# Filling the first block of a two-layer fp32 transformer kernel tile by tile instead of by column halves

## The reference

```
def swiglu(x, w_gate, w_up, w_down):
    return (jax.nn.silu(x @ w_gate) * (x @ w_up)) @ w_down

f1 = swiglu(rms_norm(x, ffn1_pre_g[l]), ffn1_w_gate[l], ffn1_w_up[l], ffn1_w_down[l])
x = x + FFN_RESIDUAL_WEIGHT * rms_norm(f1, ffn1_post_g[l])
m = token_mixer(rms_norm(x, mix_pre_g[l]), w_in[l], ...)
x = x + rms_norm(m, mix_post_g[l])
f2 = swiglu(rms_norm(x, ffn2_pre_g[l]), ffn2_w_gate[l], ffn2_w_up[l], ffn2_w_down[l])
```

## Time and profile before

| what | value |
|---|---|
| median of three runs | 1047.85 us (1047.4 to 1048.85) |
| the profiled execution's own time | 1048.85 us |
| its span | 1047.0 us |
| PE busy | 1030.4 us, 98% |
| DVE busy | 629.5 us, 60% |
| ACT busy | 473.7 us, 45% |
| DMA over the span | 178.78 MB, mean 171 GB/s |

### The profile page before, as it was taken

The page is one execution under the profiler, slowest core; times in us unless marked ns, Lnnn a source line. Parts: engine busy times, 40 slices in busy tenths (PEclk is TensorE's granted clock), DMA queues, the critical chain, the costliest instruction groups (busy, mean ns, idle before and its releaser), DMA issues.

```text
span 1047.0 us, 13589 instructions
## 1 busy us (share of the span) xinstructions
PE 1030.4 (98%) x5026; PEld 855.5 (82%) x5026; DVE 629.5 (60%) x642; ACT 473.7 (45%) x537; POOL 69.8 (7%) x81
## 2 busy tenths in 40 slices
PE   8999999999979999999999999999999999999998
PEld 6888888778867888888888888888888888888887
DVE  6555456655556645455664478876777766544553
ACT  6534445555453634443544542335446445434342
POOL 2000000100110100000010002243000000000000
PEclk9999999999999999999999999999999999999999
DMA  9755657565313455655646543334436555565551
GB/s 311 233 192 184 200 163 230 178 198 176 121 41 120 148 194 180 200 162 198 231 152 201 179 148 116 121 121 153 129 121 201 162 200 190 176 197 190 194 177 41
DMA packets 116664, 178.78 MB, mean 171 GB/s; under 512 B 5640, under 2 KB 73488, under 8 KB 116496
## 3 DMA queue, kind: packets, MB, share of 16 engines
q1 hardware_dynamic: 115808, 174.82, 51.0%
q0 software_dynamic: 512, 1.71, 0.6%
q10 hardware_dynamic: 304, 1.70, 0.6%
HBM read 177.15 MB, written 2.63 MB: 172 GB/s over the span
## 4 chain that ended last, share of the span: by engine, by line
PE 94%; DVE 3%; ACT 2%; issue 1%; DMA 0%; POOL 0%; SPq 0%; ACTq 0%; DVEq 0%; POOLq 0%
PE gu L492 14%; PE gu L493 14%; PE gu L494 14%; PE acc L492 10%; PE acc L494 10%; PE acc L493 10%; PE tp L492 3%; PE tp L494 3%; PE tp L493 3%; PE acc L819 3%; PE tp L631 1%; PE gu L734 1%; PE acc L720 1%; PE tp L533 1%; PE acc L746 1%
## 5 line engine op out<-in xcount | busy, mean ns | idle before, releaser
L1504 DVE TENSOR_TENSOR wlo<-raw,whi 128x2048 fp32r<-128x2048 f32 x149 | 346.1, 2326 | 188.7 <-ACT whi L1018 188.0
L1018 ACT ACTIVATE whi<-raw 128x2048 fp32r<-128x2048 f32 x150 | 286.3, 1912 | 146.3 <-PE acc L494 93.7
L492 PE MATMUL gu<-whi,act_hi 128*128 128x512 f32 x592 | 235.0, 397 | 0.0
L493 PE MATMUL gu<-wlo,act_hi 128*128 128x512 f32 x592 | 230.9, 390 | 0.0
L494 PE MATMUL gu<-whi,act_lo 128*128 128x512 f32 x592 | 230.7, 390 | 0.0
L494 PEld LDWEIGHTS gu<-whi,act_lo 128*128 128x128 f32 x592 | 111.2, 188 | 23.9
L492 PEld LDWEIGHTS gu<-whi,act_hi 128*128 128x128 f32 x592 | 111.2, 188 | 22.9 <-DVE act_lo L1521 0.5
L493 PEld LDWEIGHTS gu<-wlo,act_hi 128*128 128x128 f32 x592 | 111.3, 188 | 21.6
L492 PE MATMUL acc<-whi,hT_hi 128*128 128x512 f32 x240 | 93.7, 390 | 0.0
L494 PE MATMUL acc<-whi,hT_lo 128*128 128x512 f32 x240 | 93.5, 389 | 0.0
L493 PE MATMUL acc<-wlo,hT_hi 128*128 128x512 f32 x240 | 93.4, 389 | 0.0
(11 more groups left out here) (272 smaller groups left out, 1352.0 us busy)
## 6 DMA issues: line engine op xcount, KB each, us to landing
raw<-in_w_in SPq DMA_DIRECT2D x96, 512.0 KB, 4.5
raw<-in_down SPq DMA_DIRECT2D x66, 512.0 KB, 4.0
raw<-in_gate SPq DMA_DIRECT2D x64, 512.0 KB, 4.0
raw<-in_up SPq DMA_DIRECT2D x64, 512.0 KB, 4.9
raw<-in_w_out SPq DMA_DIRECT2D x16, 512.0 KB, 4.7
raw<-in_w_branch_hg SPq DMA_DIRECT2D x8, 512.0 KB, 4.3
raw<-in_w_branch_attn SPq DMA_DIRECT2D x8, 512.0 KB, 4.7
post<-in_post_gains SPq DMA_DIRECT2D x3, 512.0 KB, 5.5
```

The source lines that it names most:

```text
L492: pe.matmul(out, hi, w_hi, start=start, stop=False)
L493: pe.matmul(out, hi, w_lo, start=False, stop=False)
L1018: act.activation(split_weights(k)[0], raw[:, k % RING, :], ACT.Copy).then_inc(hi_ready, 1)
L1504: dve.tensor_tensor(w_lo, raw[:, k % RING, :], w_hi.bitcast(F32), ALU.subtract).then_inc(lo_ready, 1)
```

## The change

Three things change, all in the opening.

The turns of the first stage go by tile: turn 1 now takes tile 0, half 1, and turn 2 takes tile 1, half 0. `x_in[i]` is the semaphore of tile and half in that order, so it is the same number as the turn.

The part of x that turn 1 needs is loaded by ACT, right behind `fixed`. On SP the half piece 0b moves ahead of tile 1's first half.

PE, ACT and DVE take the opening in another order: five warm-up products before the turns (seven before), none between turns 0 and 1 (two before), six behind turn 1 (three before). Turn 2 stands behind the four products of piece 0 and tile 0, and PE waits for it at once. Turn 3 stands behind the first product of tile 1.

```
-FILLS = [BY_HALF if u in (T_FFN1, T_WOUT, T_WOUT2) else BY_TILE for u in range(9)]
+FILLS = [BY_HALF if u in (T_WOUT, T_WOUT2) else BY_TILE for u in range(9)]
             def first_pieces():
                 x_part(0, 0)
                 half_piece(0, 0)
+                half_piece(0, 1)
                 x_part(1, 0)
-                half_piece(0, 1)
-                x_part(0, 1)
                 half_piece(1, 0)
                 x_part(1, 1)
                 half_piece(1, 1)
...
-                warm_up(7)
+                warm_up(5)
                 pe.wait_ge(head_in, 16)
                 turn(0)
-                warm_up(2)
                 turn(1)
-                warm_up(3)
+                warm_up(6)
                 filled(u, 1)
                 for a in range(4):
                     if a < 3:
...
                         pe.wait_ge(lo_ready, 1)
                     product(0, 0, a)
-                    if a == 1:
-                        turn(2)
+                turn(2)
+                filled(u, 3)
+                product(0, 1, 0)
+                turn(3)
+                for a in range(1, 4):
+                    mm = product(0, 1, a)
+                mm.then_inc(piece_used, 1)
                 filled(u, 2)
-                for a in range(4):
-                    mm = product(0, 1, a)
-                    if a == 1:
-                        turn(3)
-                mm.then_inc(piece_used, 1)
-                filled(u, 3)
                 pe.wait_ge(part_lo, 4)
...
             act.dma_start(fixed[:, 0:G_END + P], fixed_d[:, 0:G_END + P]).then_inc(head_in, 16)
+            act.dma_start(x[:, 0, BLK:D], x_d[0:P, BLK:D]).then_inc(x_in[1], 16)
             act.wait_ge(pool_step, 1)
             load_table(0, ACT.Silu)
-            first_hi(0, 0, 1)
             fills(T_FFN1, 0)
-            for a in range(1, 4):
+            for a in range(4):
                 first_hi(0, a, 1)
-            fills(T_FFN1, 1)
+            fills(T_FFN1, 1, 2)
             first_hi(1, 0, 2)
-            fills(T_FFN1, 2)
+            fills(T_FFN1, 3)
+            first_hi(1, 2, 2)
             x_sums(0, 0)
-            first_hi(1, 2, 2)
-            fills(T_FFN1, 3)
             hi(2)
...
             fill_scaled(T_FFN1, 0)
-            first_lo(0, 0, 1)
+            fill_scaled(T_FFN1, 1)
             fill_rest(T_FFN1, 0)
-            first_lo(0, 1, 1)
-            fill_scaled(T_FFN1, 1)
-            first_lo(0, 2, 1)
-            first_lo(0, 3, 1)
+            for a in range(4):
+                first_lo(0, a, 1)
+            fill_scaled(T_FFN1, 2)
             fill_rest(T_FFN1, 1)
-            fill_scaled(T_FFN1, 2)
-            first_lo(1, 0, 2)
             fill_rest(T_FFN1, 2)
             fill_scaled(T_FFN1, 3)
+            first_lo(1, 0, 2)
+            fill_rest(T_FFN1, 3)
             first_lo(1, 2, 2)
-            fill_rest(T_FFN1, 3)
             lo(2)
```

More of the change, by code:

```diff
@@ L560, in turn @@
                 def turn(i):
-                    t, h = FILLS[u][i]
-                    pe.wait_ge(x_in[2 * t + h], 16)
+                    pe.wait_ge(x_in[i], 16)
                     fill(u, i, from_x)
```

## The result

The changed kernel takes 1053.5 us (median of 5 runs, 1053.24 to 1053.89) against 1047.85. The ratio to the kernel before is 1.0051, 95% interval 1.0037 to 1.0066. The sign was forecast (slower, 0.87), the size was not: +2.9 us was the sum, +5.65 came, and 1053.5 lies 0.5 above the upper end of the range.

What follows compares the result with a forecast made beforehand. PE's list was taken to bound the kernel: 2.5 us for tile 1's first product plus 0.4 for the second half of wlo made +2.9, so 1047.85 + 2.9 = 1050.8 us, range 1049.4 to 1053.0.

Steps and rivals of the forecast that it cites:

- What bounds the kernel: Whole kernel: PE, busy 98% of the span, sets the time, with no slack behind the opening to absorb a delay.
- DMA: Opening loads: 0a lands at 6.9, 0b keeps 8.55, tile 0's second half lands at 5.6; a second issuer saves only issue time.
- A: Landing of tile 0's second half of x in the opening, taken as 5.6 us between bounds 5.0 and 6.9.
- free queue: Rival in the opening: ACT's transfer uses spare DMA room, 0b up to 0.7 us earlier; +2.3, 1050.2 us; chance 0.10.
- Start of the products: Opening: PE starts products at 8.35 against 8.28, the fourth ends near 11.4, and fewer early warm-up products cost nothing.
- The new wait: Behind turn 2: PE stands through its conversion, 2.8 us with 2.3 idle; tile 1's first product comes 2.5 us later.
- Behind it: Rest of the first block: 0.4 us waiting for the second wlo half, L864 at 23.3, +2.9; next block covered.
- the first rival: Behind the new wait the clock falls to half for up to 3.4 us of products; +4.2, 1052.1 us; chance 0.30.
- the 0.4 of waiting: First block, behind turn 3: PE waits 0.4 us for the second half of wlo of piece 1.
- Not slower: Rival in the attention stage: its clock no longer falls, winning back 1.7 us; +1.2, 1049.1 us; chance 0.10.
- The base: Starting point of the forecast: the kernel before at its median of 1047.85 us, to which 2.9 us was added.

Runs made afterwards that it cites:

- i1: The kernel before with thirty unread products filling the attention-stage wait behind the turned weights of pair 4; 1050.2 us, ratio 1.0006.
- i3: The kernel before with 9, 3 and 3 warm-up products and thirty unread products in the attention-stage wait; 1048.98 us, ratio 0.9996.
- g1: The kernel before with only tile 1's first half of x issued by ACT instead of SP; 1049.14 us, ratio 1.0005.
- f5: The changed kernel with 9, 2 and 3 warm-up products and nine more in the wait behind turn 2; 1053.14 us, ratio 1.0035.
- f6: The changed kernel with 9, 2 and 3 warm-up products, the wait behind turn 2 left empty; 1053.51 us, ratio 1.0041.
- e4: The kernel before with only the changed kernel's warm-up products (5, 0, 6); 1051.95 us, ratio 1.0023.
- h: The changed kernel run once more, unedited, beside other runs; 1054.01 us, ratio 1.0045 to the kernel before.
- i2: The changed kernel with thirty unread products in the attention-stage wait; 1054.44 us, ratio 1.0039.
- e1: The changed kernel with the warm-up products of the kernel before (7, 2, 3); 1054.6 us, ratio 1.0042.
- f7: The kernel before with 9, 3 and 3 warm-up products; 1049.14 us, ratio 0.9994.
- g2: The kernel before with only DVE's scaling of turn 1 moved ahead of the first wlo quarter; 1052.18 us, ratio 1.0017.
- f8: The changed kernel with 9, 2 and 3 warm-up products and turn 2 back between the second and third product; 1051.7 us, ratio 1.0020.
- g3: The kernel before with first up piece from ACT's queue, turn 0 converted ahead of whi, warm-up 9, 3 and 1; 1050.01 us, ratio 1.0004.
- e2: The changed kernel with nine unread warm-up products in the wait behind turn 2; 1053.96 us, ratio 1.0040.
- e3: The changed kernel with turn 2 back between the second and third product of piece 0; 1052.65 us, ratio 1.0028.

## Why the prediction went wrong, step by step

*What bounds the kernel: right.* The delay of the opening went through to the attention stage whole (218.5 to 218.6 us from the end of the block in every profile). What differs behind that is falls of the clock and, in i1 to i3, the late piece.

*DMA: right in kind, A too early.* In the first profile turn 1 used the second half of tile 0 at 5.77, near the forecast 5.6. In five others of the new order it stood at 6.07 to 6.46, behind an idle time that `x` ended, so the near hit was luck of that run. Piece 0a came later by using ACT's queue (7.05 in g1 against 6.27). The prediction's sign of a free queue, 0b's `whi` before 8.2, did show in the first profile, at 7.98, but f5 and f6 have 8.61 and 8.46. The windows say what the second queue brought: with the new order 1.59 to 1.65 MB had moved by 7 us, with the old one 1.47 to 1.55, and by 9 us the difference was down to some 0.05. In g1, with the old order and a second issuer, it was 1.46 by 7 us. The Trainium skill's rule ("DMA: Bandwidth & Descriptors", section "Issuing engines are not separate DMA queues") fits g1, where the second issuer moved no more bytes; whether order or issuer gave the little more of the new order was not tested.

*Start of the products: the step that failed.* "Five warm-up products in place of seven, and none between the turns, cost nothing on this path, since PE waits there for DMA" looked only at time, and not at what the products do to the clock. With five, the clock is at 1.2 GHz until about 9.4 in the first profile and about 11 at the latest (e4). Turn 1 takes 1.11 in place of 0.66, so DVE gets its scaling late and with it all four `wlo` quarters; the six products behind it take 2.77 us and overrun. The four products ended at 12.17, forecast 11.37. The edit alone, in e4, costs 2.4 us. In the changed kernel it costs less, 0.6 to 0.8 (h against f6, with and without the 0.2 by which `x` came later), since the wait for DVE lies beside most of it.

Landing A is the second miss of this step. With the clock up and the same order (f5) the first product came at 9.10, not 8.35, since turn 1 came at 6.37 and not at 5.6. The prediction's sizes on DVE held: from turn 1 to the first product it had 2.75 us, and f5 has 2.73.

*The new wait: right.* 2.77 us from turn 2 to the next product in every profile that has turn 2 late (12.17 to 14.94, 12.66 to 15.43, 11.81 to 14.58 and four more). The waits for `wlo` in the rest of the block came about as forecast: in f5, without a fall, it takes 9.36 us, forecast 8.77 + 0.4 = 9.17.

*Behind it: the first rival came true.* "What speaks against it is that the work on either side is dense" was the wrong weight. The clock fell behind the wait in both profiles of the changed kernel, in f6 and in i2, not in e1's. Priced at 1.7 less the 0.4 of waiting, it cost 1.1 (f6 against f5) to 1.31 (the split above). So the rival's size was right and its chance, 0.30, too low: the sum that the forecast rests on ran the products behind the wait at the full clock. The Trainium skill ("TensorE: Matmul & The Clock Gate", section "Why this matters for your kernels") warns of idle gaps between bursts of products, but only of longer ones; here 2.17 us was enough, and in the kernel before 1.96. The measurement decides. The range had room for this fall with 0.9 to spare, but not for fall and late start together.

*Not slower: half right, and rarer than the profile suggested.* In the first profile of the changed kernel the attention stage kept its clock and won back 1.1 (75.6 to 74.6 in the stage; priced 1.7). A stretch of 3.4 us at half clock takes about 0.0016 from the mean clock of a 1050-us run, so 0.998 is one such stretch and 0.997 two. Of the first six runs of the changed kernel four had 0.997: most had the second fall.

*The base.* The forecast was put on a median of three runs, at the better of the two groups of the kernel before. Against the twenty and more runs beside h the change costs 1.0045, or 4.7 us: less than 5.65, since most of those runs have a fall of their own. Like is compared with like at the end of the block, where the ladder has 5.7: the new order with turn 2 late 3.9, the fall 1.0, the late rise 0.8. (The 3.9 is also what e1's four runs give.) The forecast was 2.9. Of the 1.0 between 2.9 and 3.9, 0.6 is landing A: the four products ended at 11.94 in f5, forecast 11.37. The rest is 0.2 for `wlo` and 0.2 by which f7 ends ahead of the kernel before.

What stays open: why e1 and g1 lost the clock's early rise with the very warm-up that gave it to the kernel before, what decides whether and where the clock falls in the attention stage, and what puts single runs of the kernel before at 1050.5 and above, beyond what one fall costs, and why the piece at 851 us lands late once the attention wait is filled.

## What to carry to other kernels

Warm-up products are no padding: before cutting or moving one, ask at which clock the next real work on TensorE would run, and read that from the duration of the same instruction, not from the clock column ahead of its first change. When a change makes the matrix engine stand for 2 us, price the wait twice, once as time and once as a stretch at half clock behind it, and check by filling the wait. A transpose that others wait for belongs ahead of work that doesn't need it, since its chain through two other engines (2.77 us here) is paid in full otherwise.

## What the runs showed of the hardware

- The clock fell to half behind an idle time of 2.17 us between dense products in four profiles (0.53 over 3.42 us in the first), and not behind the same 2.17 in e1. In g2 it fell within an idle time of 2.19.
- In the attention stage an idle time of 1.95 or 1.96 had a fall right behind it in eight profiles, one some 16 us later in four, none in two. The late ones stand behind a sparse stretch whose longest idle time was 1.26 or 1.27 us. The same work has all three outcomes.
- Such a fall cost 1.1 us right behind the wait, 1.4 to 1.7 at the later place, and 1.1 to 1.3 in the opening.
- With seven warm-up products ahead of it, turn 0 ran at the full clock in the kernel before and in g2 (0.66), took 0.80 in i1, and 1.11 in g1 and e1. With nine it took 0.66 in f5, f6 and i3, 0.78 in f7, and 1.11 in f8 and g3, where turn 1 took 0.65 and 0.66: the rise lay between them. With five it took about 1.11 in all six profiles (the changed kernel, e2, e3, e4, h, i2), and so did turn 1.
- The clock column shows 1.00 for a first stretch at 1.2 GHz: 7.40 to 9.40 in the changed kernel, with warm-up products of 0.46 us.
- Covering the wait in the attention stage took away the fall right behind it (none in i1, i2 and i3), but i1 fell at 312, and a weight piece landed late at 851 us, which gave 0.85 to 1.03 us back.
